# Making the low parts of the weights on GpSimd beside the scans, in a two-layer hybrid encoder

## The chip, the cores and the metric

The kernel runs on one core of a Trainium2 chip. The metric is the device time of one execution in microseconds (us); three runs of the kernel before took 1644.47 to 1645.33 us, with a median of 1645.07 us. Lower is better.

## The reference, cut to what matters

A sequence of 512 positions with 1024 features goes through two layers. Each layer does this:

```
h = rmsnorm(x, norm1_g[i])
u = h @ w_in[i]
q, k, v, z, xbc, dt_raw, sc_b, sc_c, sc_x = split(u)
a_out = attention_mixer(q, k, v, ...)          # 8 heads, dilated windows
s_out = ssd_mixer(z, xbc, dt_raw, ...)         # 16 heads, two directions, chunks of 128
c_out = short_conv_mixer(sc_b, sc_c, sc_x, ...)
x = x + concatenate([a_out, s_out, c_out]) @ w_out[i]
x = x + conv_ffn(rmsnorm(x, norm2_g[i]), ...)  # silu(gate) * val, 2816 wide
```

The SSD mixer ends with a gate and a norm over each of two groups of heads, and the sum of squares of a group is taken over 512 features:

```
y = y.reshape(b, s, SSD_GROUPS, gsz) * silu(z).reshape(b, s, SSD_GROUPS, gsz)
y = y * rsqrt(mean(y * y, axis=-1) + EPS)
```

All of it is float32. The kernel computes the large products in three passes of a faster format: each operand is split into a high part (rounded) and a low part (what the rounding leaves), and high x high, high x low and low x high are summed.

## The kernel before, in words

Weights come in chunks of 128 x 1024 (512 KB), 128 of them a layer and a small one (dt), in one fixed order (CHUNKS): qk, dt, v, xbc, sc, z, o1 (first half of the output projection), o2 (second half), up, dn. Raw chunks W, high parts WHI and low parts WLO have two buffers each, taken in turn. SyncE loads chunk n when the low part of chunk n-2 is made. ScalarE makes the high part of chunk n+2 (L525) when TensorE has used chunk n (`high_after`). Another engine then makes the low part, raw minus high, and counts it in the semaphore w_lo. TensorE waits for w_lo before a chunk's first matmul and then runs 24 matmuls of 512 columns, three for each of 8 blocks (L1168 to L1170).

The 28 chunks sc, z and o1 are the slots 0 to 27 (SLOTS). Beside them the scans of the SSD run, and each engine's program goes through the slots in the same order and places pieces of the scan there by slot number. Each engine is an in-order queue: an instruction that waits holds up all behind it. The pieces that matter here:

- sc slots 0 to 11: three slots make one tile of the short convolution. VectorE adds two taps (L1093, on SBUF alone), multiplies (L1069, L1071), ScalarE makes the product's high part (L710) and GpSimd its low part (L488) in slots 2, 5, 8 and 11.
- Scan groups start in slots 2 and 13. TensorE turns the group's tiles into token order, ScalarE copies them out (L734), GpSimd scales them (`scale_states`, L462, two in each of three slots), TensorE makes states of them (L1318).
- Heads: DMA brings a head's rows, ScalarE makes the decays (`head_exp`, L609, L612), VectorE weighs them (L915) and adds the two directions (L920, on SBUF alone) in slots 4 to 11 and 15 to 22. TensorE uses two heads at a time (`within`, L1330), in slots 6, 8, 10, 12, 17, 19, 21 and 23. After it VectorE combines (`combine`, L924, L931, L932) and GpSimd adds the backward part (`add_backward`, L467).
- z slots 12 to 19: VectorE evacuates z tile i into one of four buffers (L1078); from z4 on it waits until GpSimd's `gate` (L472) of tile i-4 has read that buffer. Gates 0 and 1 stand in slot 16, 2 and 3 in slot 17, 4 to 6 in slots 20 to 22, 7 in slot 24.
- Sums of squares: GpSimd adds four squared tiles to one (`sum_squares`, L450 and L452), for group 0 in slot 24 and for group 1 in slot 27. TensorE sums over the partitions (L1217): for group 0 after slot 25, and for group 1 within the first o2 chunk, between its two halves.

In all other chunks GpSimd makes the low part (L437). In the 28 slots VectorE makes it (L845), at the place of `low_after` in VectorE's slot loop: after the evacuation and the weighing, before `combine` and the taps. In GpSimd's loop over o2 the first low part waits for the last one of VectorE.

Of the kernel before, what the change touches and what calls it, by code (L numbers as in the profile page):

```python
# [8 lines left out]
F32, F32R = mybir.dt.float32, mybir.dt.float32r  # L9
ACT, ALU = mybir.ActivationFunctionType, mybir.AluOpType  # L10
# [56 lines left out]
NCH = len(CHUNKS)  # L67
POS = {c: i for i, c in enumerate(CHUNKS)}
# [76 lines left out]
def build_trunk(nc, a):  # L145
    ctx = ExitStack()
    now = [0]

    def sb(name, shape, dt=F32):
        return ctx.enter_context(nc.sbuf_tensor(f"sb_{name}", shape, dt))  # L150
# [13 lines left out]
    def sem(name, per=0):  # L164
        return Count(ctx.enter_context(nc.semaphore(name)), per, now)
# [6 lines left out]
    W = sb("w_raw", [P, 2, CHUNK])  # L172
    WHI = sb("w_hi", [P, 2, CHUNK], F32R)
    WLO = sb("w_lo", [P, 2, CHUNK], F32R)
# [80 lines left out]
    w_hi, w_lo, w_used = sem("w_hi", NCH), sem("w_lo", NCH), sem("w_used", NCH)  # L255
# [54 lines left out]
    def direction_chunk(j):  # L310
        d, i = j % 2, j // 2
        return d, (i if d == 0 else QT - 1 - i)
# [116 lines left out]
    def _(pool):  # L429
# [9 lines left out]
        def low_after(kind, i):  # L439

            n = now[0] * NCH + POS[kind, i] + 2
            if (kind, i) == ("o2", 0):
                pool.wait_ge(w_lo.handle, n)
            if n < DEPTH * NCH:
                w_low(n)

# [7 lines left out]
        def scale_states(n):  # L454
            grp, j = n // 6, n % 6
            d, c = direction_chunk(j)
            col = column(d, 8 * grp)
            pool.wait_ge(*ws_done.at(1))
            pool.wait_ge(*tok_copied.at(5 * grp + 5))
            if j >= 2:  # L460
                pool.wait_ge(*st_mm.at(n - 1))
            g.tensor_tensor(SQ[:, j % 2, :].rearrange("p (h e) -> p h e", e=64), XT[:, c, :].rearrange("p (h e) -> p h e", e=64),  # L462
                            WS[:, c, col:col + 8].unsqueeze(2).to_broadcast([P, 8, 64]), ALU.mult).then_inc(xs_done.handle, 1)
# [12 lines left out]
        for layer in range(DEPTH):  # L476
            now[0] = layer
            for pos in range(POS["sc", 0]):
                low_after(*CHUNKS[pos])
                if layer == 0 and CHUNKS[pos] == ("qk", 2):  # L480
                    pool.wait_ge(bias_row.handle, 2)
                    g.dma_start(scratch[:, :, :], rm["bias_row"][:, :].unsqueeze(1).to_broadcast([HEADS, COPIES, REL]))\
                        .then_inc(bias_stored.handle, 16)
            for s, (kind, i) in enumerate(SLOTS):
                if kind == "sc" and i % 3 == 2:
                    t = i // 3
                    pool.wait_ge(*sc_hi.at(t + 1))
                    g.tensor_tensor(rm["ml_sc"][:, t, :], SCP[:, :], rm["mh_sc"][:, t, :].bitcast(F32), ALU.subtract)\  # L488
                        .then_inc(sc_lo.handle, 1)
                for grp in range(SSD_GROUPS):  # L490
                    if 0 <= s - GROUP_AT[grp] < 3:
                        for j in range(2):
                            scale_states(6 * grp + 2 * (s - GROUP_AT[grp]) + j)
                if s in PAIR_AT:
                    add_backward(PAIR_AT[s])
                if s in (16, 17):
                    gate(2 * (s - 16))
                    gate(2 * (s - 16) + 1)
                if s in (20, 21, 22):
                    gate(s - 16)  # L500
                if s == 24:
                    gate(7)
                if s in (24, 27):
                    sum_squares((s - 24) // 3)
            for m in range(KT):
                low_after("o2", m)
            for j in range(2 * FF_T):
                low_after("up", j)
                if j % 2 == 1:
                    t = j // 2  # L510
                    pool.wait_ge(*ff_hi.at(t + 1))
                    g.tensor_tensor(FLO[:, t, :], FP[:, :], FHI[:, t, :].bitcast(F32), ALU.subtract).then_inc(ff_lo.handle, 1)  # L512
            for i in range(DOWN_C * KT):
                low_after("dn", i)
# [290 lines left out]
    def _(dve):  # L805
        v = nc.vector
# [30 lines left out]
            v.scalar_tensor_tensor(mixed("l", 8 + t), XC[:, t, :], par(PA_SNG + t), mixed("h", 8 + t).bitcast(F32),  # L837
                                   ALU.mult, ALU.subtract).then_inc(y_lo.handle, 1)

        def low_after(kind, i):  # L840

            n = now[0] * NCH + POS[kind, i] + 2
            dve.wait_ge(w_hi.handle, n + 1)
            dve.wait_ge(w_lo.handle, n)
            v.tensor_tensor(WLO[:, n % 2, :], W[:, n % 2, :], WHI[:, n % 2, :].bitcast(F32), ALU.subtract).then_inc(w_lo.handle, 1)  # L845

        def root_ready(name):
            dve.wait_ge(*root_done.at(NORMS.index(name) + 1))

# [101 lines left out]
        for layer in range(DEPTH):  # L951
# [81 lines left out]
            for s, (kind, i) in enumerate(SLOTS):  # L1033
# [19 lines left out]
                b, n = TILE_BANK[kind, i]  # L1053
# [28 lines left out]
                if s in WEIGH_AT:  # L1082
                    weigh(WEIGH_AT[s])
                    add_directions(WEIGH_AT[s])
                low_after(kind, i)
                if s in PAIR_AT:
                    combine(PAIR_AT[s])
                if kind == "sc" and i % 3 == 1:
# [16 lines left out]
            for m in range(KT):  # L1105
                b1, n1 = TILE_BANK["o1", m]
                dve.wait_ge(*evac[b1].at(n1 + 1))
                for half in range(2):
                    b, n = TILE_BANK["o2", 2 * m + half]
# [18 lines left out]
            for j in range(2 * FF_T):  # L1128
                t, col = j // 2, PA_FF + 4 * j
                b, n = TILE_BANK["up", j]  # L1130
# [14 lines left out]
            for m in range(KT):  # L1145
                b, n = TILE_BANK["down", m]
# [419 lines left out]
```

## Time and profile before

| | |
|---|---|
| median of 3 runs | 1645.07 us |
| profiled execution | 1644.51 us (span 1642.6 us) |
| TensorE matmul busy | 1621.8 us, 99% |
| VectorE busy | 910.4 us, 55% |
| ScalarE busy | 763.3 us, 46% |
| GpSimd busy | 645.7 us, 39% |
| granted TensorE clock | 1.000 |

Busy time over span gives the share of each engine. The slots of the first layer lie between 209 and 409 us of the span, those of the second 812 us later. In that stretch (212 to 412 us) VectorE is busy 138.73 us of 200, ScalarE 125.57 and GpSimd 51.01. In the views below, a row of the timeline has its start, its length, the engine, the line and the operation with its shapes. The bracket at its end is the idle time of the engine before it, and what ended it. The times of consecutive rows of one instruction form (x2) are merged.

### The profile page before, as it was taken

What the parts mean: (1) busy time and instruction counts of PE and PEld (TensorE: products, weight loads), DVE (VectorE), ACT (ScalarE), POOL (GpSimd) and SP (SyncE); (2) the same over time, 40 slices, a digit from 0 to 9 for tenths busy, and PEclk for the clock granted to TensorE, in tenths of its full rate; (3) what the DMA queues carried; (4) which work ended last, traced back from release to release, by engine and by line L of the source; (5) the groups of instructions that cost most, each with busy time, mean ns of one, the idle gap of its engine ahead of it and who ended that gap; (6) DMA issues with size and microseconds to landing.
All of it is one profiled execution on the core that took longest, in us unless ns stands there. A gap on an engine that the chain in (4) does not pass through costs nothing.

```text
span 1642.6 us, 19275 instructions
## 1 busy us (share of the span) xinstructions
PE 1621.8 (99%) x7352; PEld 1266.6 (77%) x7352; DVE 910.4 (55%) x1310; ACT 763.3 (46%) x1204; POOL 645.7 (39%) x323
## 2 busy tenths in 40 slices
PE   7999999999999999999999999999999999999999
PEld 5776778787778888888877776787777788888887
DVE  4578858567754545421227778686678455455000
ACT  5456666575343333332244665765734433333221
POOL 3432221224345555554443322213144555555443
PEclk9999999999999999999999999999999999999999
DMA  5532145352223322323324222454523223322333
GB/s 170 133 105 80 52 115 159 126 159 91 91 90 91 102 91 90 98 87 95 93 90 129 87 74 65 129 155 131 153 83 101 91 90 90 97 96 87 96 93 109
DMA packets 57371, 170.86 MB, mean 104 GB/s; under 512 B 5984, under 2 KB 11872, under 8 KB 57280
## 3 DMA queue, kind: packets, MB, share of 16 engines
q1 hardware_dynamic: 56896, 168.88, 33.4%
q0 software_dynamic: 384, 0.75, 0.4%
q8 instruction: 59, 0.97, 0.3%
q14 instruction: 32, 0.26, 0.0%
HBM read 166.24 MB, written 3.38 MB: 103 GB/s over the span
## 4 chain that ended last, share of the span: by engine, by line
PE 85%; DMA 5%; DVE 3%; issue 3%; POOL 2%; ACT 2%; SPq 1%; DVEq 0%; POOLq 0%; ACTq 0%
PE banks L1168 25%; PE banks L1169 25%; PE banks L1170 25%; DMA sb_w_raw<-w_in 3%; PE banks L1246 2%; PE banks L1255 2%; PE banks L1266 2%; DMA sb_e<-sum_rows 1%; PE banks L1318 1%; PE banks L1226 1%; POOL sb_xc L472 1%; DVE sb_w_lo L845 1%; SPq L337 1%; ACT sb_w_hi L525 0%; DVE sb_sc_acc L1093 0%
## 5 line engine op out<-in xcount | busy, mean ns | idle before, releaser
L437 POOL TENSOR_TENSOR sb_w_lo<-sb_w_raw,sb_w_hi 128x1024 fp32r<-128x1024 f32 x200 | 482.4, 2412 | 629.3 <-ACT sb_w_hi L525 629.3
L525 ACT ACTIVATE sb_w_hi<-sb_w_raw 128x1024 fp32r<-128x1024 f32 x256 | 271.3, 1060 | 739.4 <-PE banks L1170 686.6
L1168 PE MATMUL banks<-sb_h_hi,sb_w_hi 128*128 128x512 f32 x1344 | 550.2, 409 | 12.1 <-POOL sb_w_lo L437 10.7
L1169 PE MATMUL banks<-sb_h_lo,sb_w_hi 128*128 128x512 f32 x1344 | 533.4, 397 | 0.0
L1170 PE MATMUL banks<-sb_h_hi,sb_w_lo 128*128 128x512 f32 x1344 | 533.0, 397 | 0.0
L1168 PEld LDWEIGHTS banks<-sb_h_hi,sb_w_hi 128*128 128x128 f32 x1344 | 253.6, 189 | 92.1 <-issue 29.3
L1169 PEld LDWEIGHTS banks<-sb_h_lo,sb_w_hi 128*128 128x128 f32 x1344 | 253.7, 189 | 64.3 <-issue 6.5
L1170 PEld LDWEIGHTS banks<-sb_h_hi,sb_w_lo 128*128 128x128 f32 x1344 | 253.5, 189 | 61.8
L1133 DVE TENSOR_TENSOR banks<-banks,sb_rstd 128x512 f32<-128x512 f32 x88 | 61.5, 699 | 148.9 <-PE banks L1170 139.7
L1168 PE MATMUL banks<-sb_ff_hi,sb_w_hi 128*128 128x512 f32 x352 | 139.6, 396 | 0.0
L1169 PE MATMUL banks<-sb_ff_lo,sb_w_hi 128*128 128x512 f32 x352 | 139.6, 396 | 0.0
L1170 PE MATMUL banks<-sb_ff_hi,sb_w_lo 128*128 128x512 f32 x352 | 139.5, 396 | 0.0
L1148 DVE TENSOR_TENSOR sb_x_stream<-banks,sb_x_stream 128x512 f32<-128x512 f32 x16 | 11.1, 692 | 201.2 <-PE banks L1170 201.2
L845 DVE TENSOR_TENSOR sb_w_lo<-sb_w_raw,sb_w_hi 128x1024 fp32r<-128x1024 f32 x56 | 72.7, 1298 | 25.5 <-ACT sb_w_hi L525 25.4
L1170 PEld LDWEIGHTS banks<-sb_ff_hi,sb_w_lo 128*128 128x128 f32 x352 | 66.3, 188 | 16.2
L1169 PEld LDWEIGHTS banks<-sb_ff_lo,sb_w_hi 128*128 128x128 f32 x352 | 66.3, 188 | 16.2
L1168 PEld LDWEIGHTS banks<-sb_ff_hi,sb_w_hi 128*128 128x128 f32 x352 | 66.3, 188 | 16.2
L512 POOL TENSOR_TENSOR sb_ff_lo<-sb_ff_prod,sb_ff_hi 128x512 fp32r<-128x512 f32 x44 | 56.9, 1292 | 51.5 <-DVE sb_ff_hi L1144 51.5
L868 DVE SCALAR_TENSOR_TENSOR sb_xc<-banks,sb_params,sb_xc 128x509 f32<-128x509 f32 (+2 forms) x96 | 71.9, 749 | 5.5 <-ACT sb_xc L582 2.6
L467 POOL TENSOR_TENSOR sb_xc<-sb_xc,sb_t_normed 128x384 f32<-128x384 f32 x16 | 18.9, 1183 | 139.0 <-DVE sb_xc L932 139.0
L894 DVE CUSTOM_DVE_ANT_0 sb_scores<-banks,sb_bias_t 128x512 f32<-128x512 f32 x64 | 41.5, 685 | 33.0 <-PE banks L1246 33.0
L1135 DVE SCALAR_TENSOR_TENSOR sb_ff_val<-banks,sb_params,sb_ff_val 128x511 f32<-128x511 f32 x44 | 33.0, 750 | 46.2 <-ACT sb_ff_val L786 46.2
(206 smaller groups left out, 2220.5 us busy)
## 6 DMA issues: line engine op xcount, KB each, us to landing
sb_w_raw<-w_in SPq DMA_DIRECT2D x88, 512.0 KB, 3.7
sb_w_raw<-w_up SPq DMA_DIRECT2D x88, 512.0 KB, 3.6
sb_w_raw<-w_out SPq DMA_DIRECT2D x32, 512.0 KB, 3.6
sb_w_raw<-w_down SPq DMA_DIRECT2D x32, 512.0 KB, 3.5
sb_e<-sum_rows SPq DMA_DIRECT2D x16, 512.0 KB, 6.1
sb_bias_t<-bias_rows SPq DMA_DIRECT2D x16, 448.0 KB, 5.9
sb_exp_cs<-sum_rows SPq DMA_DIRECT2D x32, 192.0 KB
sb_w_raw<-w_down SPq DMA_DIRECT2D x16, 384.0 KB, 3.2
```

The source lines that it names most:

```text
L437: g.tensor_tensor(WLO[:, n % 2, :], W[:, n % 2, :], WHI[:, n % 2, :].bitcast(F32), ALU.subtract).then_inc(w_lo.handle, 1)
L512: g.tensor_tensor(FLO[:, t, :], FP[:, :], FHI[:, t, :].bitcast(F32), ALU.subtract).then_inc(ff_lo.handle, 1)
L525: sc.activation(WHI[:, n % 2, :], W[:, n % 2, :], ACT.Copy).then_inc(w_hi.handle, 1)
L845: v.tensor_tensor(WLO[:, n % 2, :], W[:, n % 2, :], WHI[:, n % 2, :].bitcast(F32), ALU.subtract).then_inc(w_lo.handle, 1)
L868: ins = v.scalar_tensor_tensor(acc[:, lo:hi], src[:, lo + o:hi + o], par(PA_CONV7 + 8 * n + t), acc[:, lo:hi], ALU.mult, ALU.add)
L894: v.tensor_tensor_reduce(S[:, u % 2, :], bank(2 + u % 2), BIAS[:, h % 4, at:at + SEQ], scale=-1.0, scalar=3e38, op0=ALU.add, op1=ALU.min, ...
L1133: v.tensor_tensor(bank(b), bank(b), RSTD, ALU.mult).then_inc(up_scaled.handle, 1)
L1135: step(v.scalar_tensor_tensor(acc[:, 1:SEQ], BANK[:, b, 0:SEQ - 1], par(col), acc[:, 1:SEQ], ALU.mult, ALU.add))
L1168: mm(out, whi, hhi, start=start, stop=False)
L1169: mm(out, whi, hlo, start=False, stop=False)
L1170: return mm(out, wlo, hhi, start=False, stop=stop)
L1246: ins = mm(bank(2 + u % 2), qs[hs, h // 2, P * qt:P * qt + P], ks[hs, h // 2, :], start=n == 0, stop=n == 2)
```

## The change

In the 28 slots GpSimd makes the low parts, with the same subtraction. VectorE's function for it and its call go. In GpSimd's slot loop the call stands after the short convolution's low part (sb_ml_sc) and the state scalings, and ahead of `add_backward`, of the gates and of the sums of squares. The wait of GpSimd for VectorE's last low part goes too, since all low parts are now counted by one engine.

```diff
@@ gpsimd
         def low_after(kind, i):
 
             n = now[0] * NCH + POS[kind, i] + 2
-            if (kind, i) == ("o2", 0):
-                pool.wait_ge(w_lo.handle, n)
             if n < DEPTH * NCH:
                 w_low(n)
@@
                         for j in range(2):
                             scale_states(6 * grp + 2 * (s - GROUP_AT[grp]) + j)
+                low_after(kind, i)
                 if s in PAIR_AT:
                     add_backward(PAIR_AT[s])
@@ vector
-        def low_after(kind, i):
-
-            n = now[0] * NCH + POS[kind, i] + 2
-            dve.wait_ge(w_hi.handle, n + 1)
-            dve.wait_ge(w_lo.handle, n)
-            v.tensor_tensor(WLO[:, n % 2, :], W[:, n % 2, :], WHI[:, n % 2, :].bitcast(F32), ALU.subtract).then_inc(w_lo.handle, 1)
-
@@
                     weigh(WEIGH_AT[s])
                     add_directions(WEIGH_AT[s])
-                low_after(kind, i)
                 if s in PAIR_AT:
                     combine(PAIR_AT[s])
```

Line numbers of the changed kernel are up to two lower on GpSimd (L450 is L448 there) and up to ten lower on VectorE and after it. First the GpSimd queue from slot 0 to slot 5 of the first layer, before (sb_w_lo is a low part of weights, sb_ml_sc the short convolution's low part, sb_squares a scaled state; x18 and x20 begin in the chunks before the slots):

```order
L437 TENSOR_TENSOR sb_w_lo<-sb_w_raw,sb_w_hi 128x1024 x18
L488 TENSOR_TENSOR sb_ml_sc<-sb_sc_prod,sb_mh_sc 128x512
L462 TENSOR_TENSOR sb_squares<-sb_x_tok,sb_state_weights 128x512 x6
L488 TENSOR_TENSOR sb_ml_sc<-sb_sc_prod,sb_mh_sc 128x512
L467 TENSOR_TENSOR sb_xc<-sb_xc,sb_t_normed 128x384
```

And the same place in the changed kernel:

```order
L437 TENSOR_TENSOR sb_w_lo<-sb_w_raw,sb_w_hi 128x1024 x20
L486 TENSOR_TENSOR sb_ml_sc<-sb_sc_prod,sb_mh_sc 128x512
L460 TENSOR_TENSOR sb_squares<-sb_x_tok,sb_state_weights 128x512 x2
L437 TENSOR_TENSOR sb_w_lo<-sb_w_raw,sb_w_hi 128x1024
L460 TENSOR_TENSOR sb_squares<-sb_x_tok,sb_state_weights 128x512 x2
L437 TENSOR_TENSOR sb_w_lo<-sb_w_raw,sb_w_hi 128x1024
L460 TENSOR_TENSOR sb_squares<-sb_x_tok,sb_state_weights 128x512 x2
L437 TENSOR_TENSOR sb_w_lo<-sb_w_raw,sb_w_hi 128x1024
L486 TENSOR_TENSOR sb_ml_sc<-sb_sc_prod,sb_mh_sc 128x512
```

A low part now follows each pair of scaled states, and the one of slot 5 follows the second sb_ml_sc. Next GpSimd's queue from the second group's scaled states to gates 2 and 3, slots 13 to 17, before (sb_xc with sb_z is a gate, sb_xc with sb_t_normed an add_backward, sb_sq_ssd the sums of squares):

```order
L462 TENSOR_TENSOR sb_squares<-sb_x_tok,sb_state_weights 128x512 x6
L472 TENSOR_TENSOR sb_xc<-sb_xc,sb_z 128x512 x2
L467 TENSOR_TENSOR sb_xc<-sb_xc,sb_t_normed 128x384
L472 TENSOR_TENSOR sb_xc<-sb_xc,sb_z 128x512 x2
```

The same place in the changed kernel, from the last two scaled states on (slots 15 to 17):

```order
L460 TENSOR_TENSOR sb_squares<-sb_x_tok,sb_state_weights 128x512 x2
L437 TENSOR_TENSOR sb_w_lo<-sb_w_raw,sb_w_hi 128x1024 x2
L470 TENSOR_TENSOR sb_xc<-sb_xc,sb_z 128x512 x2
L437 TENSOR_TENSOR sb_w_lo<-sb_w_raw,sb_w_hi 128x1024
L465 TENSOR_TENSOR sb_xc<-sb_xc,sb_t_normed 128x384
L470 TENSOR_TENSOR sb_xc<-sb_xc,sb_z 128x512 x2
```

The low parts of slots 15 and 16 stand ahead of gates 0 and 1. Last, slots 24 to 27 on GpSimd, before:

```order
L472 TENSOR_TENSOR sb_xc<-sb_xc,sb_z 128x512
L450 TENSOR_TENSOR sb_sq_ssd<-sb_sq_ssd 128x1024
L452 TENSOR_TENSOR sb_sq_ssd<-sb_sq_ssd 128x512
L450 TENSOR_TENSOR sb_sq_ssd<-sb_sq_ssd 128x1024
L452 TENSOR_TENSOR sb_sq_ssd<-sb_sq_ssd 128x512
```

And in the changed kernel:

```order
L437 TENSOR_TENSOR sb_w_lo<-sb_w_raw,sb_w_hi 128x1024
L470 TENSOR_TENSOR sb_xc<-sb_xc,sb_z 128x512
L448 TENSOR_TENSOR sb_sq_ssd<-sb_sq_ssd 128x1024
L450 TENSOR_TENSOR sb_sq_ssd<-sb_sq_ssd 128x512
L437 TENSOR_TENSOR sb_w_lo<-sb_w_raw,sb_w_hi 128x1024 x3
L448 TENSOR_TENSOR sb_sq_ssd<-sb_sq_ssd 128x1024
L450 TENSOR_TENSOR sb_sq_ssd<-sb_sq_ssd 128x512
```

One low part stands ahead of gate 7 and the first sum of squares, and three (slots 25, 26 and 27) between the two sums.

## Rows read from the trace of the kernel before

**Rows 1.** TensorE's waits over the span: total us, times, longest

```profile
PE banks L1168 <- POOL sb_w_lo L437: 10.7, 2, 10.0
PE banks L1217 <- POOL sb_sq_ssd L452: 2.9, 2, 1.7
PE banks L1330 <- DVE sb_squares L920: 1.3, 2, 0.8
```

**Rows 2.** The page's part 5: the two lines that make low parts

```profile
L437 POOL TENSOR_TENSOR sb_w_lo<-sb_w_raw,sb_w_hi 128x1024 fp32r<-128x1024 f32 x200 | 482.4, 2412 | 629.3 <-ACT sb_w_hi L525 629.3
L845 DVE TENSOR_TENSOR sb_w_lo<-sb_w_raw,sb_w_hi 128x1024 fp32r<-128x1024 f32 x56 | 72.7, 1298 | 25.5 <-ACT sb_w_hi L525 25.4
```

**Rows 3.** Timeline of GpSimd and VectorE, slot 22: start us, us

```profile
378.57 2.98 POOL L472 TENSOR_TENSOR sb_xc<-sb_xc,sb_z 128x512 f32<-128x512 f32 x2
380.35 2.29 DVE L845 TENSOR_TENSOR sb_w_lo<-sb_w_raw,sb_w_hi 128x1024 fp32r<-128x1024 f32 x1
```

**Rows 4.** Timeline of GpSimd, ScalarE and TensorE, end of slot 27

```profile
404.48 2.92 POOL L450 TENSOR_TENSOR sb_sq_ssd<-sb_sq_ssd 128x1024 f32<-128x1024 f32 x1 [8.49 <-ACT sb_sq_ssd L559]
407.47 1.63 POOL L452 TENSOR_TENSOR sb_sq_ssd<-sb_sq_ssd 128x512 f32<-128x512 f32 x1
408.45 1.06 ACT L525 ACTIVATE sb_w_hi<-sb_w_raw 128x1024 fp32r<-128x1024 f32 x1 [4.05 <-PE banks L1170]
411.05 1.02 PE L1217 MATMUL banks<-sb_sq_ssd,sb_constants 128*128 128x512 f32 x2
```

**Rows 5.** Timeline of ScalarE, GpSimd and TensorE, slots 21 to 25

```profile
371.42 1.04 ACT L525 ACTIVATE sb_w_hi<-sb_w_raw 128x1024 fp32r<-128x1024 f32 x1
382.87 0.51 PE L1168 MATMUL banks<-sb_mh_at,sb_w_hi 128*128 128x512 f32 x1
388.79 1.06 ACT L525 ACTIVATE sb_w_hi<-sb_w_raw 128x1024 fp32r<-128x1024 f32 x1 [3.31 <-PE banks L1170]
389.68 1.29 POOL L472 TENSOR_TENSOR sb_xc<-sb_xc,sb_z 128x512 f32<-128x512 f32 x1
396.04 1.13 PE L1217 MATMUL banks<-sb_sq_ssd,sb_constants 128*128 128x512 f32 x2 [1.66 <-POOL sb_sq_ssd L452]
```

**Rows 6.** Timeline of ScalarE, VectorE and TensorE, slots 16 and 17

```profile
333.06 1.06 ACT L525 ACTIVATE sb_w_hi<-sb_w_raw 128x1024 fp32r<-128x1024 f32 x1
334.36 0.68 DVE L1078 TENSOR_TENSOR sb_z<-banks,sb_rstd 128x512 f32<-128x512 f32 x1
336.20 0.69 DVE L920 TENSOR_TENSOR sb_e<-sb_e 128x512 f32<-128x512 f32 x1
338.59 1.06 ACT L525 ACTIVATE sb_w_hi<-sb_w_raw 128x1024 fp32r<-128x1024 f32 x1 [0.94 <-PE banks L1170]
339.82 1.09 PE L1330 MATMUL banks<-sb_e,sb_x_tok 128*64 128x128 f32 x16
```

**Rows 7.** Timeline of ScalarE, VectorE, GpSimd and TensorE, slots 1 to 4

```profile
224.03 1.06 ACT L525 ACTIVATE sb_w_hi<-sb_w_raw 128x1024 fp32r<-128x1024 f32 x1
226.27 1.53 DVE L1093 SCALAR_TENSOR_TENSOR sb_sc_acc<-sb_sc_cx,sb_params,sb_sc_acc 128x511 f32<-128x511 f32 x2
232.51 2.04 POOL L462 TENSOR_TENSOR sb_squares<-sb_x_tok,sb_state_weights 128x512 f32<-128x512 f32 x2 [0.96 <-ACT sb_x_tok L734]
237.19 0.40 PE L1169 MATMUL banks<-sb_h_lo,sb_w_hi 128*128 128x512 f32 x1
```

**Rows 8.** Timeline of ScalarE and TensorE, slots 8 and 10; second layer's landing

```profile
275.33 1.06 ACT L525 ACTIVATE sb_w_hi<-sb_w_raw 128x1024 fp32r<-128x1024 f32 x1 [4.42 <-DMA sb_w_raw<-w_in]
279.20 0.39 PE L1168 MATMUL banks<-sb_h_hi,sb_w_hi 128*128 128x512 f32 x1
1086.78 1.06 ACT L525 ACTIVATE sb_w_hi<-sb_w_raw 128x1024 fp32r<-128x1024 f32 x1 [3.58 <-DMA sb_w_raw<-w_in]
```

**Rows 9.** Timeline of TensorE, tenth and last matmul; last stretch of the windows

```profile
13.90 0.40 PE L1168 MATMUL banks<-sb_h_hi,sb_w_hi 128*128 128x512 f32 x1
1639.04 0.39 PE L1170 MATMUL banks<-sb_ff_hi,sb_w_lo 128*128 128x512 f32 x1
1642.00:1642.60 0.60, 0.00 (x0) 0.00 (x0) 0.00 (x0) 0.00 (x0) 0.00 (x0) 0.50 0.00 0
```

## The prediction

> **What bounds the kernel now.** I read the page first. TensorE is busy 99% of the span, and the chain that ended last is 85% TensorE. So almost nothing can be won, and what counts is how often TensorE would stand still. Its waits come next [rows 1]: beside 10.0 us before the first matmul, they are 2.9 us on GpSimd's sums of squares (L452) and 1.3 us on VectorE's L920, both in the scans. The change acts only in the 28 slots of a layer in which a projection chunk is computed beside the scans (slots 0 to 11 sc, 12 to 19 z, 20 to 27 o1). I therefore walked GpSimd's new queue through these slots, with the durations of the timeline, and asked at each step whether TensorE would be waiting. In the sc and z slots a chunk takes about 5.6 us, and each low part must be there when its chunk begins, one slot and the scan's matmuls later.
>
> **What the change removes, adds and moves.** Of the 256 chunks, 56 low parts leave VectorE (28 a layer, 1.30 us each by the mean) and go to GpSimd, 2.41 us each [rows 2]. That is 36 us a layer off VectorE and 67 us a layer onto GpSimd. Both engines have room for it on average, and by that alone the answer would be "nothing". What decides is that queues run in order, and GpSimd's queue holds instructions that wait. Two things are new. A low part now stands behind the scan's work on GpSimd, or that work stands behind the low part, which waits for its high part (w_hi), which ScalarE makes only when TensorE is done with the slot. The w_lo waits that go were free of charge. The DMAs are unchanged, but SyncE loads chunk n+2 when low part n is done, so that late low parts make late loads.
>
> **GpSimd and VectorE shut each other out.** GpSimd's two gates ran from 378.57 to 381.55, and VectorE's low part, issued at 380.35, took 2.29 us and ended at 382.64, 1.09 us after the gate [rows 3]. So it did its work only after GpSimd's instruction. Operations with a PSUM operand show no such stretch. The Trainium skill says so too and speaks against the change: by its page "SBUF — State Buffer", section "SBUF: two separate sides", a VectorE instruction with two SBUF inputs and a GpSimd instruction that reads SBUF exclude each other for the whole instruction. The trace agrees, with the 1.09 us. Were it a mere sharing, or nothing, term 3 below would be 0.6 us instead of 2.9 and the first part of term 4 near 0, some 7 us less in all. A GpSimd instruction that holds this for 2.4 us is twice as long a lock as the one removed.
>
> **Term 1, sum of squares of group 1: +5.5 us a layer.** Before, L450 started at 404.48 and L452 ended at 409.10, and TensorE took the sum at 411.05 without waiting [rows 4]. Now three low parts stand ahead of it; the last belongs to slot 27, whose high part starts at 408.45 and ends at 409.51 [rows 4]. Low part 2.4 gives 411.98; then 2.92 and 1.63 with 0.1 between: 416.6. TensorE comes at 411.05: 5.5 us of waiting. I see no cover for it; the second half of the output matmuls stands behind this sum in its queue.
>
> **Term 2, sum of squares of group 0: +3.9 us.** In slot 21 the high part ends at 372.46 [rows 5], the low part on GpSimd at 374.9, and VectorE's L920 waits for it. Then the add_backward behind the combination (2.5 us of VectorE, 1.0 of GpSimd), gate 5 (1.3), L920 of the next head (0.6) and the next low part (2.4) end at about 383.9, where the chunk of slot 24 began at 382.87 [rows 5]: 1.0 us. In slot 24 the high part starts at 388.79, 1.0 later now: 389.8; behind it 1.06, low part 2.4, gate 1.29 [rows 5], then 2.92 and 1.63, and gaps of 0.3: 399.4, with one VectorE instruction let in between (0.7) about 400. TensorE took this sum at 396.04 after 1.66 us of waiting [rows 5]. So +3.9 (bounds 3.3 and 4.3).
>
> **Term 3, the gates: +2.9 us.** Slot 16's low part stands ahead of gates 0 and 1. Its high part ends at 334.12 [rows 6], the low part at 336.6, gate 0 at 337.9. VectorE's evacuation of z4 (334.36 before) waits for gate 0, since both use the same buffer: it starts at 338.0, and L920 of head 9 is issued 1.84 us later, as 334.36 and 336.20 show [rows 6]: 339.8. But the next high part ends at 339.64 [rows 6], so that GpSimd's low part starts at 339.7, a tenth ahead, and shuts L920 out until 342.1; it ends at 342.7. TensorE needs it at 339.82 [rows 6]: 2.9. If VectorE comes first, 340.4, and the term is 0.6. I take 2.9, as GpSimd is a hair earlier, and keep 0.6.
>
> **Term 4, the sc slots: +2.4 us in the first layer, about 1.8 in the second.** In slot 1 the high part ends at 225.09, GpSimd holds until 227.5, and VectorE's two taps (226.27 before) start 1.2 late; behind them are the product, ScalarE's high part of it and its token copies, and then the two state scalings on GpSimd, 232.51 to 234.55 before [rows 7], now to 235.7. The low part of slot 2 stands behind these: 238.2. TensorE then passes its second matmul at 238.5, not 237.19 [rows 7]: +1.35. In slot 8 the chunk lands with the high part at 275.33 [rows 8]; this landing is late because DMA queues are full behind row loads that wait for TensorE, so I shift it by 1.7 with slot 4's delay and SyncE's order. Then 1.06 for the high part, 0.6 for ScalarE's product, 1.3 for the sc low part in front, 2.4 and gaps: 282.4. The chunk began at 279.1 (its second matmul of the next triple is 279.20) and would now begin at 280.6 [rows 8]: +1.85. Of these 3.2 us, 0.8 is taken back where TensorE waited for L920 before [rows 1]. In the second layer the landing is 0.8 earlier against the slots (1086.78 less 812.3 is 274.5 [rows 8]), but its tile before began as late, hence about 1.8. Bounds: 0, if the loads hold TensorE up anyway, and 3.3.
>
> **The clock.** TensorE ran its first matmuls from 10.00 and reached the 0.24 us spacing at 13.90 after nine of them [rows 1, 9]. At that spacing nine take 2.1 us, so a cold start costs 1.8. The last matmul starts at 1639.04, and the granted clock is 0.50 (1.2 GHz of 2.4) in the last stretch, from 1642.0 [rows 9]. So idling of under 3 us can take it down. Terms 1 and 2 make gaps of 5.5 and, with the wait that is there, 4 to 5 us. I charge one drop a layer, 1.8; bounds none and two.
>
> **Sum.** A layer: 5.5 + 3.9 + 2.9 = 12.3; two are 24.6; the sc slots 4.2; two drops 3.6: 32.4 us. What VectorE gains (36 us a layer) hides beside TensorE, apart from the 0.8 counted above. The profiled execution took 1644.51 (span 1642.6), 0.6 below the median of the runs, 1645.07: 1644.5 + 32.4 = 1676.9, against the median 1677. As such a walk on paper tends to count waits that overlap, I name 1676.
>
> **Rivals.**
> A: only the end of the scans costs. The races go to VectorE (0.6), the sc slots are bounded by their loads (0), and the clock holds: 2 x (5.5 + 3.3 + 0.6) = 18.8, 1664. For it: the sc low parts had up to 2 us of room; against: the slot 2 chain has no load in it.
> B: the clock falls in both gaps of each layer, and the terms are at their upper bounds: 2 x (5.5 + 4.3 + 2.9 + 3.3 + 3.6) = 39, 1684.
> C, faster: VectorE was what held TensorE (L920 1.3 us, and its low parts), and its relief reaches TensorE because GpSimd's three low parts are finished before their turn. This decides if the sum of squares of group 1 isn't delayed, by less than 1.9 us: then 2 x 1.1 us are won, 1642. Against it stands rows 4: the high part of slot 27 ends after the old sums did.
> D: nothing moves, 1645: late low parts and sums are all absorbed by TensorE's queue. The same row is against it.
>
> **Chances.** My case 0.60, A 0.20, B 0.14, C 0.03, D 0.03. The range 1660 to 1686 takes in A and B and leaves out C, D and a part of the tails. A change of 0.2% (3.3 us) is about what can be told from none: faster 0.02, same 0.03, slower 0.95.
>
> **What would show it.** The wait of L1217 on GpSimd's L450 line: 5.5 us a layer for group 1 and some 5 for group 0, where all was 2.9 in total. The z4 evacuation on VectorE waits for GpSimd's gate, with L920 of 2 to 3 us behind it. GpSimd's low parts number 256 at 2.4 us, VectorE's are none. TensorE waits for w_lo in slots 4 and 10, 1 to 2 us. After the two sums of a layer matmuls spaced 0.43 us tell of the clock. I am wrong if L1217 waits under 2 us in group 1, or if the low parts of slots 25 to 27 end before the sum begins without delaying it.

## The result, and the profile of the changed kernel

The changed kernel takes 1681.68 us (median of 4 runs, 1678.51 to 1682.47), the kernel before 1644.77 us beside it (median of 4 runs, 1643.22 to 1645.33). The ratio is 1.0223, with an interval of [1.0209, 1.0238]: 36.9 us slower. The prediction named 1676 us and the range 1660 to 1686.

The page's head and its part 1 say at once that nothing is short of capacity:

```profile
span 1680.6 us, 19217 instructions
PE 1636.5 (97%) x7352; PEld 1274.7 (76%) x7352; DVE 883.4 (53%) x1254; ACT 763.7 (45%) x1204; POOL 773.4 (46%) x379
L437 POOL TENSOR_TENSOR sb_w_lo<-sb_w_raw,sb_w_hi 128x1024 fp32r<-128x1024 f32 x256 | 621.7, 2429 | 745.5 <-ACT sb_w_hi L524 745.5
```

GpSimd has all 256 low parts at 2.4 us, as expected (the last row, from part 5, answers to [rows 2]; VectorE's row is gone), and it is still idle for more than half of the span. What changed is how often TensorE stands still. Its waits (engine, line, waited for: total us, times, longest) answer to [rows 1]; line numbers of the changed kernel are 9 lower for TensorE and 2 lower for GpSimd behind the removed wait, and up to 8 lower for VectorE (L920 is L912 there, and L837 is L836):

```profile
PE banks L1159 <- POOL sb_w_lo L437: 18.2, 9, 10.7
PE banks L1208 <- POOL sb_sq_ssd L450: 15.6, 4, 4.4
PE banks L1321 <- DVE sb_e L912: 5.6, 2, 2.8
```

Before these were 10.7, 2.9 and 1.3 us. The new 24.5 us are 12.7 at the sums of squares, 4.3 at the last operation of a head, and 7.5 at low parts. A row of the kernel before has nothing left to answer to it, since VectorE makes no low parts now:

```profile
PE banks L1168 <- DVE sb_w_lo L845: 1.5, 2, 1.1
```

These two waits were in slot 23 of each layer (0.37 and 1.10 us). The new waits stand where the timeline of TensorE has them (start, us, and in brackets the wait ahead; the last row is of the second layer):

```profile
239.07 0.50 PE L1159 MATMUL banks<-sb_h_hi,sb_w_hi 128*128 128x512 f32 x1 [0.89 <-POOL sb_w_lo L437]
283.36 0.50 PE L1159 MATMUL banks<-sb_h_hi,sb_w_hi 128*128 128x512 f32 x1 [1.77 <-POOL sb_w_lo L437]
347.54 1.09 PE L1321 MATMUL banks<-sb_e,sb_x_tok 128*64 128x128 f32 x16 [2.78 <-DVE sb_e L912]
...
407.26 2.08 PE L1208 MATMUL banks<-sb_sq_ssd,sb_constants 128*128 128x512 f32 x2 [3.33 <-POOL sb_sq_ssd L450]
428.37 2.08 PE L1208 MATMUL banks<-sb_sq_ssd,sb_constants 128*128 128x512 f32 x2 [4.44 <-POOL sb_sq_ssd L450]
...
1115.18 0.50 PE L1159 MATMUL banks<-sb_h_hi,sb_w_hi 128*128 128x512 f32 x1 [2.20 <-POOL sb_w_lo L437]
```

Waits alone don't make up 38.0 us, the difference of the two spans. The rest is the clock. These are windows right behind five of those waits (last three columns: granted clock, DMA share, GB/s):

```profile
283.60:287.00 3.40, 3.40 (x10) 2.69 (x10) 3.37 (x2) 3.37 (x10) 3.01 (x2) 0.58 0.79 236
348.90:352.40 3.50, 3.50 (x10) 2.71 (x9) 3.33 (x6) 0.00 (x0) 0.00 (x0) 0.51 0.39 117
407.60:411.00 3.40, 3.40 (x8) 1.99 (x8) 2.91 (x2) 1.60 (x3) 2.36 (x1) 0.58 0.04 5
428.80:432.40 3.60, 3.60 (x8) 2.08 (x8) 0.00 (x0) 1.32 (x2) 0.00 (x0) 0.50 0.00 0
1115.40:1118.80 3.40, 3.40 (x16) 2.72 (x16) 3.37 (x2) 3.37 (x10) 3.07 (x2) 1.00 0.78 238
```

PE is busy in all of the window and still does 8 to 10 matmuls where it does 16 at full clock: it ran at 1.2 GHz instead of 2.4. The last window, behind the wait of slot 10 in the second layer, kept the full clock. How many such stretches there are differs between executions of the same kernel: the mean granted clock of the four was 0.991, 0.992, 0.991 and 0.994, and the time followed it. The profiled one is the slowest of the four (1682.47 us).

To see which step costs what, take the same matmul in both traces and subtract the starts. Where this shift grows, time is lost. For each layer, in us, with the start that the matmul had before:

| place | what grows it | layer 1 | layer 2 | both |
|---|---|---|---|---|
| slots 0 to 13 (199.7 to 301) | waits at slots 4 and 10, less the old wait at L920 (0.9 and 0.7) | 1.99 | 2.94 | 4.9 |
| slot 17 (339.82) | VectorE's L912 is late | 2.85 | 2.86 | 5.7 |
| slots 21 to 25 (up to 396.04) | slot 24's start, sum of group 0, less the old wait for VectorE's low part in slot 23 (0.0 and 1.0) | 1.97 | 1.50 | 3.5 |
| slot 27 (411.05) | sum of group 1 | 4.44 | 4.45 | 8.9 |
| behind those gaps | matmuls at 1.2 GHz | 7.84 | 6.12 | 14.0 |

That is 37.0 us. The table's last row is what remains of the shift when the waits are taken off. Another 1.1 us arises in the first 200 us, ahead of anything that the change touches; the kernels of the experiments have 0.1 to 1.0 there, so it is scatter.

### The profile page after: what moved, and what is told of

Its sections match the earlier page's. It is cut to its first block, busy times and chain, and to the rows that moved or that the text cites. A ratio compares the mean times of both kernels' runs of the same rounds, so it can differ in the third digit from the quotient of the medians.

```text
span 1680.6 us, 19217 instructions
## 1 busy us (share of the span) xinstructions
PE 1636.5 (97%) x7352; PEld 1274.7 (76%) x7352; DVE 883.4 (53%) x1254; ACT 763.7 (45%) x1204; POOL 773.4 (46%) x379
## 4 chain that ended last, share of the span: by engine, by line
PE 85%; POOL 4%; DVE 3%; ACT 3%; issue 2%; DMA 2%; SPq 0%; DVEq 0%; POOLq 0%; ACTq 0%
PE banks L1159 25%; PE banks L1160 25%; PE banks L1161 25%; DMA sb_w_raw<-w_in 2%; POOL sb_w_lo L437 2%; PE banks L1237 2%; PE banks L1246 2%; PE banks L1257 2%; PE banks L1217 1%; PE banks L1309 1%; POOL sb_sq_ssd L448 1%; PE banks L1321 1%; POOL sb_squares L460 1%; PE banks L1335 0%; PE banks L1208 0%
## 5 line engine op out<-in xcount | busy, mean ns | idle before, releaser
L437 POOL TENSOR_TENSOR sb_w_lo<-sb_w_raw,sb_w_hi 128x1024 fp32r<-128x1024 f32 x256 | 621.7, 2429 | 745.5 <-ACT sb_w_hi L524 745.5
L819 DVE SCALAR_TENSOR_TENSOR sb_h_lo<-sb_x_stream,sb_params,sb_h_hi 128x512 fp32r<-128x512 f32 x32 | 50.1, 1589 | 16.5 <-ACT sb_h_hi L535 16.5
L1126 DVE SCALAR_TENSOR_TENSOR sb_ff_gate<-banks,sb_params,sb_ff_gate 128x511 f32<-128x511 f32 x44 | 33.0, 750 | 45.8 <-ACT sb_ff_gate L785 45.8
```

What stands on the lines that cost most here:

```text
L437: g.tensor_tensor(WLO[:, n % 2, :], W[:, n % 2, :], WHI[:, n % 2, :].bitcast(F32), ALU.subtract).then_inc(w_lo.handle, 1)
L819: v.scalar_tensor_tensor(HLO[:, k, :], X[:, k, :], par((PA_N1, PA_N2)[norm] + k), HHI[:, k, :].bitcast(F32), ALU.mult, ALU.subtract).then_ ...
L1126: step(v.scalar_tensor_tensor(acc[:, 1:SEQ], BANK[:, b, 0:SEQ - 1], par(col), acc[:, 1:SEQ], ALU.mult, ALU.add))
```

## The experiments

All times are medians; ratios are to the kernel before, run on the same chip. What an experiment gives back is worked out from the ratios, and each carries an interval of about 0.15%, 2.5 us, on either side. Slots and terms are the prediction's.

**Slot 27's low part behind the sum (term 1).**

```
+                if s != 27:
                     low_after(kind, i)
 ...
                     sum_squares((s - 24) // 3)
+                if s == 27:
+                    low_after(kind, i)
```

> The changed kernel, with the low part of slot 27 behind the sum of squares of group 1 on GpSimd instead of ahead of it. My theory (the sum waits for a low part that can't be made before TensorE is done with slot 27): TensorE's wait of 4.4 us at this sum goes in both layers, with the stretch at 1.2 GHz behind it, 8.4 us a layer of shift against the kernel before; the rest stays. Time about 1665 us, ratio to the kernel before 1.012. Rival (GpSimd is simply too full, and work that is put off comes back later): the wait moves to the low part of the second o2 chunk, and the time falls by less than 4 us.

Measured: 1667.38 us, ratio 1.0151 [1.0135, 1.0166]. TensorE's waits on the sums fall to two of 3.3 us: those of group 1 are gone. Against the change's 1.0223 it gives back 0.72%, 11.8 us, where I expected 16.8. The waits went as expected (4.4 us a layer), but in this trace a half-clock stretch stands behind slot 10 in both layers and a double one behind the first layer's sum of group 0, so that only two of nine stretches are saved.

**Only slot 27's low part on GpSimd, all else as before.**

```
+ON_GPSIMD = (27,)
 ...
+            if slot == len(SLOTS) or slot in ON_GPSIMD:
                 pool.wait_ge(w_lo.handle, n)
 ...
+                if s in ON_GPSIMD:
+                    low_after(kind, i)
 ...
```

VectorE's call stays for all other slots. The further experiments that start from an `ON_GPSIMD` line have the same edit around it.

> The kernel before with one low part a layer (slot 27's) on GpSimd, ahead of the sum of squares of group 1. My theory: that one instruction carries term 1: high part ends at 409.5, low part 2.4, sums 2.34 and 1.26: TensorE waits 4.4 us, and 1.7 more in a half-clock stretch behind; 2 x 6.1 = 12.2, 1657 us, ratio 1.0075. Rival 1: the queue of the three low parts of slots 25 to 27 makes the wait, and one alone costs 0 to 2 us a layer: 1645 to 1649. Rival 2: the clock falls only because of other gaps before it in the layer: 1653.5, ratio 1.0055.

Measured: 1658.04 us, ratio 1.0084 [1.0069, 1.0099], 13.8 us. Two of 256 low parts make more than a third of the whole loss. GpSimd's timeline of this kernel shows why:

```profile
409.05 2.37 POOL L438 TENSOR_TENSOR sb_w_lo<-sb_w_raw,sb_w_hi 128x1024 fp32r<-128x1024 f32 x1 [13.66 <-ACT sb_w_hi L529]
411.39 2.34 POOL L452 TENSOR_TENSOR sb_sq_ssd<-sb_sq_ssd 128x1024 f32<-128x1024 f32 x1
413.80 1.26 POOL L454 TENSOR_TENSOR sb_sq_ssd<-sb_sq_ssd 128x512 f32<-128x512 f32 x1
```

The engine has been idle for 13.66 us, the last 5 of them with the sum's inputs ready (before, the sum began at 404.48 [rows 4]), because the low part stands first in the queue and waits for its high part. The wait at the sum is 4.5 us in each layer, as with all three low parts: rival 1 is out. So is rival 2: no wait of over 1.2 us comes ahead of it in the layer, and the granted clock from 416 to 423 is 0.67.

**Slot 16's low part behind the gates (term 3).**

```
+                if s != 16:
                     low_after(kind, i)
 ...
                     gate(2 * (s - 16) + 1)
+                if s == 16:
+                    low_after(kind, i)
```

> The changed kernel, with gates 0 and 1 ahead of the low part of slot 16. My theory (z4's evacuation waits for gate 0, and L912 behind it is then shut out by the low part of slot 17): TensorE's wait of 2.8 us at L1321 in slot 17 goes in both layers, and the half-clock stretch behind it, together some 4.3 us a layer; time about 1673 us, ratio 1.017. Rival (the wait comes from ScalarE's table loads or the heads' DMA): the wait stays at 2 us or more. If the gap was only filled by slack that another wait takes, the time moves by under 3 us.

Measured: 1673.21 us, ratio 1.0185 [1.017, 1.02]: 6.3 us back, where I expected 8.6. No wait at VectorE's L912 (L915 in this kernel) is left among TensorE's waits.

**Slot 17's low part on VectorE; slot 16's still ahead of the gates.** This separates delay from lock.

```
+ON_GPSIMD = [s for s in range(28) if s != 17]
```

> The change in every slot but 17, whose low part stays on VectorE, behind its product of head 9. This tells the exclusion apart from the mere delay by slot 16's low part, which still stands ahead of gates 0 and 1. My theory: the wait of 2.8 us for VectorE's last operation of head 9 is a lock held by GpSimd's low part of slot 17; without that low part the operation runs as soon as its product is there and TensorE waits 0.3 to 0.9 us; the half-clock stretch behind goes too: 1681.7 - 2 x 2.2 - 2.7 = 1674.6, ratio 1.018. Rival: slot 16's low part ahead of the gates is the whole cause; the wait stays 2.5 us or more and the time 1680 to 1682.

Measured: 1675.82 us, ratio 1.0195 [1.0178, 1.0212]: 4.6 us back, where I expected 7.1, and the interval just touches that of the change. What decides is therefore the trace. In the changed kernel, the same three steps on VectorE and GpSimd are:

```profile
343.44 1.21 DVE L907 TENSOR_TENSOR sb_e<-sb_e,banks 128x1024 f32<-128x1024 f32 x1
344.59 2.34 POOL L437 TENSOR_TENSOR sb_w_lo<-sb_w_raw,sb_w_hi 128x1024 fp32r<-128x1024 f32 x1 [0.61 <-ACT sb_w_hi L524]
344.69 2.79 DVE L912 TENSOR_TENSOR sb_e<-sb_e 128x512 f32<-128x512 f32 x1
```

and in this experiment (VectorE's timeline; L919 and L924 are the L907 and L912 above):

```profile
341.46 1.21 DVE L919 TENSOR_TENSOR sb_e<-sb_e,banks 128x1024 f32<-128x1024 f32 x1
342.70 0.69 DVE L924 TENSOR_TENSOR sb_e<-sb_e 128x512 f32<-128x512 f32 x1
```

GpSimd came 0.10 us ahead, and the 0.69 us operation took 2.79: it ran when GpSimd's was over (344.59 + 2.34 = 346.93, plus 0.55). Without that low part beside it, it takes 0.69, and TensorE's wait falls from 2.8 to 0.7 us in both layers. The rival, mere delay, is out: slot 16's low part only moves VectorE's work next to GpSimd's, and the lock makes the wait. The Trainium skill says in its page "SBUF — State Buffer", section "SBUF: two separate sides", that a VectorE instruction with two SBUF inputs and a GpSimd instruction that reads SBUF exclude each other for the whole instruction. The trace agrees, with 2.79 against 0.69.

**Low parts on VectorE in slots 0 to 15 (term 4).**

```
+ON_GPSIMD = range(16, 28)
```

> Low parts on VectorE in slots 0 to 15 as before, on GpSimd in slots 16 to 27 as after the change: term 4 (the sc slots) taken away alone. My theory: the sc slots cost 3.8 us in layer 1 and 3.0 in layer 2 (shift of TensorE's matmuls between slot 0 and slot 16, with the half-clock stretch behind slot 10), all else stays: 1681.7 - 6.8 = 1675 us, ratio 1.018. Rival: the late low parts of the sc slots only use up slack that the loads of the next slots take anyway, or the gates and sums take it back: 1680 to 1682, ratio 1.022.

Measured: 1673.46 us, ratio 1.018 [1.0165, 1.0196]. TensorE's matmuls have no further shift up to slot 11 (0.97 at 203.47 and at 284.82). The loads didn't take the gain back.

**Sum of group 0 first in slot 24 (term 2).**

```
+                if s == 24:
+                    sum_squares(0)
                 low_after(kind, i)
 ...
-                if s in (24, 27):
-                    sum_squares((s - 24) // 3)
+                if s == 27:
+                    sum_squares(1)
```

> The changed kernel with the sum of squares of group 0 first in slot 24 on GpSimd, all else as in the change: term 2 alone. My theory: TensorE's wait of 3.3 us there and the half-clock stretch behind it (0.5 us) go, 3.8 us a layer of which 1.7 and 1.2 were there before the change: 1681.7 - 7.4 = 1674.3, ratio 1.0185. Rival: the low part of slot 24, now 3.6 us later, is late for the next chunk and the wait comes back there as one on w_lo: 1679 to 1682.

Measured: 1671.37 us, ratio 1.0169 [1.0155, 1.0182]: 8.9 us less than the change, 1.5 more than I expected. TensorE waits for the sum of group 0 nowhere, and the low part behind it isn't late. The surplus is within the interval. The clock may have a part in it: I had counted 0.5 us of slow matmuls behind this wait, the changed kernel lost 1.5 us there in the first layer (407.60 to 411.00 above) and 2.8 in the second, and this trace has six slow stretches where that of the change has nine.

**All three: low parts first in the queue, except slot 16's behind the gates and slot 27's behind the sum.**

```
+                if s not in (16, 27):
+                    low_after(kind, i)
                 if kind == "sc" and i % 3 == 2:
 ...
-                low_after(kind, i)
```

> The changed kernel, with the low part ahead of the short convolution's low part and of the state scalings, behind gates 0 and 1 in slot 16, and behind the sum of squares in slot 27; slot 24 as in the changed kernel. My theory: the waits in slots 4, 10, 17 and at the group 1 sum go, in all about 8.4 + 4.4 + 3.5 us a layer of the 18.5; what stays is the group 0 sum, some 2 us a layer more than before. Time about 1649 us, ratio 1.003. Rival (the exclusion of VectorE by twice as long instructions costs everywhere): 1658 us or more, with new waits on VectorE's lines.

Measured: 1658.17 us, ratio 1.0093 [1.0076, 1.011], 9 us more than I expected. TensorE's timeline has the reasons:

```profile
236.05 1.16 PE L1305 MATMUL banks<-sb_bc 128*128 128x128 f32 x8 [1.00 <-ACT sb_x_tok L738]
262.52 1.09 PE L1326 MATMUL banks<-sb_e,sb_x_tok 128*64 128x128 f32 x16 [1.54 <-DVE sb_e L917]
...
401.41 2.08 PE L1213 MATMUL banks<-sb_sq_ssd,sb_constants 128*128 128x512 f32 x2 [3.33 <-POOL sb_sq_ssd L450]
```

The wait at the sum of group 0 (the last row) was expected to stay. The first two rows are new, 2.5 us in each layer, and with the half-clock stretch behind the sum of group 0 they make up most of the 9 us. With the low parts ahead of the scan's work in slots 2 to 5, chunks are in time, but the steps of the scan run beside GpSimd's low parts. Ahead of the first wait the two taps of the short convolution took 2.28 and 2.76 us beside two low parts, instead of 0.75 each. VectorE's timeline ahead of the second wait shows the stretch, L943 twice with L946 between:

```profile
253.77 2.77 DVE L943 TENSOR_TENSOR sb_t_normed<-sb_s_in,sb_decays 128x512 f32<-128x512 f32 x1
256.57 0.69 DVE L946 TENSOR_TENSOR sb_s_in<-banks,sb_t_normed 128x512 f32<-128x512 f32 x1
257.18 0.68 DVE L943 TENSOR_TENSOR sb_t_normed<-sb_s_in,sb_decays 128x512 f32<-128x512 f32 x1
```

L943 reads two operands in SBUF and took 2.77 us beside a low part, 0.68 without; L946, with one in PSUM, kept 0.69. So what came is the rival that I had named, in its time (1658) and in its sign (a new wait at a line of VectorE), though only in the sc slots. Putting the low parts first takes term 4's waits away and puts others of similar length in their place.

**The gap at the sum of group 1 filled, not shortened.** Five dummy matmuls into the sum's bank stand ahead of TensorE's wait; their result is overwritten.

```
-            pe.wait_ge(*y_tree.at(2 * grp + 2))
 ...
+                for k in range(5):
+                    mm(bank(6), con["ones"], BC[:, k % 4, :], start=True, stop=True)
+            pe.wait_ge(*y_tree.at(2 * grp + 2))
```

> The changed kernel, with five further float32 matmuls (into the bank of the sum, which overwrites them) while TensorE waits for the group 1 sum of squares: 0.86 us each, 4.3 us, about as long as the wait. My theory (idle TensorE loses its clock, and the matmuls behind the wait run at 1.2 GHz): the granted clock stays at 1.00 behind the sum, and 1.5 to 2.9 us a layer come back; time about 1677 us, ratio 1.0195. Rival (the clock falls for some other reason, or such matmuls don't hold it): clock and time stay, or the time rises by up to 0.8 us a layer.

Measured: 1677.12 us, ratio 1.0208 [1.0192, 1.0223], with runs from 1673.44 to 1679.97. In TensorE's timeline the dummies take the place of the wait:

```profile
421.47 4.45 PE L1208 MATMUL banks<-sb_bc,sb_constants 128*128 128x512 f32 x10
426.11 1.13 PE L1210 MATMUL banks<-sb_sq_ssd,sb_constants 128*128 128x512 f32 x2 [0.18 <-POOL sb_sq_ssd L450]
```

and the windows behind it and behind the sum of group 0, which was left as it is:

```profile
404.00:407.40 3.40, 2.29 (x4) 1.19 (x5) 3.40 (x2) 0.20 (x1) 3.40 (x2) 0.58 0.00 0
424.60:430.00 5.40, 5.22 (x19) 3.12 (x18) 0.00 (x0) 1.32 (x2) 1.38 (x2) 1.00 0.10 40
```

The sum comes just as late, but TensorE goes on at 2.4 GHz: it is idling, not the late sum, that brings the clock down. The other traces bear this out: a gap of 4.4 or 4.5 us stands at this sum 12 times in them, each time with a half-clock stretch behind it, and neither of the two filled gaps has one. What that is worth in time is not shown. The ratios differ by 0.15%, 2.5 us, where I expected 4.7, and their intervals overlap. The trace is of the fastest of the four runs (1673.44), in which two gaps of the second layer that were not filled (2.78 and 3.43 us) kept the clock too.

**Before, with the sum of group 0 ahead of gate 7.** No low part is moved.

```
-                if s == 24:
-                    gate(7)
                 if s in (24, 27):
                     sum_squares((s - 24) // 3)
+                if s == 24:
+                    gate(7)
```

> The kernel before, with no low part moved; in slot 24 GpSimd makes the sum of squares of group 0 ahead of gate 7 instead of behind it. My theory: this removes most of the wait of 1.66 and 1.2 us at the scan's first sum: 1642, ratio 0.9982. Rival: gate 7 comes 4 to 5 us later and holds ScalarE's high part of tile 7 and all behind it, so the gain is given back: 1644 to 1646, ratio 1.000.

Measured: 1640.51 us (11 runs), ratio 0.9982 [0.9973, 0.9991]. This is faster than both kernels, by 0.18% against the one before. That one had 2.9 us of waiting there [rows 1], which the order of one queue made. TensorE waits nowhere for the late gate.

**The same, with slot 10's low part alone on GpSimd.**

```
+ON_GPSIMD = (10,)
```

> As the kernel with the sum of squares of group 0 ahead of gate 7, and besides the low part of slot 10 alone on GpSimd: there VectorE's low part waits for a late high part and holds the combination and the product of the next head behind it. My theory: TensorE's wait of 0.76 and 0.6 us in slot 12 goes too: 1640.7, ratio 0.9974. Rival: GpSimd's 2.4 us low part makes the load of the chunk two slots on later by 1.2 us and costs as much as it brings: same time as without it, 1642. A second rival: it makes it slower, 1645, as every low part of the sc slots does in the changed kernel.

Measured: 1640.4 us (11 runs), ratio 0.998 [0.9972, 0.9989]: no difference from the last. The waits on L920 in slot 12 (0.38 and 0.35 us in the trace of the last kernel) are gone, and in the first layer TensorE waits for the low part itself instead:

```profile
293.75 0.50 PE L1173 MATMUL banks<-sb_h_hi,sb_w_hi 128*128 128x512 f32 x1 [0.46 <-POOL sb_w_lo L438]
```

The time is that of the first rival. Its mechanism, a later load, isn't seen: the wait is for the longer low part. Nor is it shown that moving this low part took the waits on L920 away. The two kernels above with GpSimd's low parts in slot 27 alone and in slots 16 to 27 leave slot 10's on VectorE and had at most 0.15 us of them, so these waits also go without such a move.

**GpSimd makes the low parts of slots 12 to 27, its queue in a mended order.** The sum of group 0 stands first in slot 24, slot 16's low part behind the gates, slot 27's behind the sum of group 1.

```
+ON_GPSIMD = range(12, 28)
 ...
+                if s == 24:
+                    sum_squares(0)
+                if s in ON_GPSIMD and s not in (16, 27):
+                    low_after(kind, i)
 ...
+                if s == 27:
+                    sum_squares(1)
+                    low_after(kind, i)
```

> Low parts on VectorE in slots 0 to 11, on GpSimd in slots 12 to 27 (16 a layer, where the change has 28), with GpSimd's queue in another order: the sum of group 0 first in slot 24, slot 16's low part behind the gates, slot 27's behind the sum of group 1. My theory: what the change cost was the order of a queue and the lock it holds in the sc slots; here it costs nothing and VectorE's relief brings nothing beyond what the early sum of group 0 brings alone: 1640 to 1642, ratio 0.998. Rival 1: the lock (16 times 2.4 us a layer instead of 1.2) costs here too, as VectorE's operations stretch: 1646 to 1650, ratio 1.003. Rival 2: the relief of VectorE (21 us a layer) brings more once nothing waits: under 1638.5, ratio below 0.997.

Measured: 1643.02 us (11 runs), ratio 0.9995 [0.9986, 1.0004]. TensorE's waits in this kernel (L929 is the L920 of the kernel before):

```profile
PE banks L1178 <- POOL sb_w_lo L438: 12.9, 5, 10.5
PE banks L1340 <- DVE sb_squares L929: 1.8, 2, 1.0
PE banks L1178 <- DVE sb_h_lo L829: 1.3, 2, 0.7
```

In the order of the change the low parts of slots 16 to 27 alone cost 1.8%; in this order those and four more a layer cost nothing against the kernel before, and about 2 us (0.13%, with intervals that overlap) against the one with the early sum of group 0. This is between my theory and rival 1. The sc slots have no such mended order among the kernels tried: the one that put their low parts first cost 0.93%. TensorE waits for no sum and no gate; what is left are two waits of 0.3 to 1.0 us a layer for low parts in the o1 slots, and one at L929. VectorE has 32 low parts fewer, and none of that reaches TensorE: rival 2 is out.

## Why the prediction was right, and where its sizes were off

The mechanism and its places were right: all the terms of the sum are seen in the trace. Terms 1 to 3 were each removed by the one reordering that they called for, term 4 by giving slots 0 to 15 back to VectorE, and the total was 1681.7 against 1676. The sizes were off in both directions.

- **What bounds it.** TensorE, and what counts is its standing still: confirmed. The prediction's list of TensorE's waits left out 1.5 us for VectorE's own low parts (the row of L845 above), and so a thing that the change could give back. By the shifts 0.9 and 0.7 us came back at L920, where 0.8 was counted for the first layer, and 0.0 and 1.0 in slot 23, where nothing was. How much of this is VectorE's relief stays open: at L920 kernels with VectorE's low parts left in place had waits from 0 to 1.0 us, and in slot 23 kernels with GpSimd's had 0.1 to 1.0.
- **Term 1, +5.5 a layer: 4.44 measured.** The sum began when the walk said (low part at 422.29, 1.1 us behind the start of its high part, which was late with all else). But it then took 2.34 + 1.26 us, where I put 2.92 + 1.63 from [rows 4]. The sizing step failed on a thing that the prediction itself explains elsewhere, the lock. VectorE's timeline of the kernel before, beside the sum from 404.48 to 409.10:

```profile
403.92 1.23 DVE L845 TENSOR_TENSOR sb_w_lo<-sb_w_raw,sb_w_hi 128x1024 fp32r<-128x1024 f32 x1 [0.40 <-ACT sb_w_hi L525]
405.06 2.89 DVE L837 SCALAR_TENSOR_TENSOR sb_ml_ssd<-sb_xc,sb_params,sb_mh_ssd 128x512 fp32r<-128x512 f32 x1
```

VectorE's low part held up the first addition until 405.15, and L837 came in ahead of the second. The change takes the low part away, and L837's operation was long done when the late sum began (416.88). GpSimd's timeline of the changed kernel:

```profile
422.29 2.38 POOL L437 TENSOR_TENSOR sb_w_lo<-sb_w_raw,sb_w_hi 128x1024 fp32r<-128x1024 f32 x1 [3.15 <-ACT sb_w_hi L524]
424.63 2.34 POOL L448 TENSOR_TENSOR sb_sq_ssd<-sb_sq_ssd 128x1024 f32<-128x1024 f32 x1
427.05 1.26 POOL L450 TENSOR_TENSOR sb_sq_ssd<-sb_sq_ssd 128x512 f32<-128x512 f32 x1
```

- **Term 2, +3.9 a layer: 1.97 and 1.50.** The same in slot 24: L448 took 2.37 us, not the 2.92 that I assumed, while L450, which VectorE's L836 still ran beside, took 1.59 as before (1.61); the 0.7 us that I added for a VectorE instruction let in did not come on top of that. Slot 24's start was late by 0.36, not 1.0: the steps that the prediction lists from 374.9 add up to 382.7, and with L920's own 0.7 us to 383.4, not to its 383.9. In the second layer slot 23 gained the 1.0 of the wait for VectorE's low part. The waits at the sum are 3.33 us against 1.66 and 1.2 before.
- **Term 3, +2.9: 2.85 and 2.86.** Right to the tenth, including who wins the race for the lock (GpSimd, by 0.10 us). With a margin so small that is luck as well: the other branch was priced at 0.6, and I took this one because GpSimd was a tenth ahead on paper too. The experiment with slot 17 on VectorE gives the other branch, 0.7 where I had written 0.6.
- **Term 4, +2.4 and 1.8: 1.99 and 2.94.** Slot 4 grew by 1.16 and 1.17 (1.35 forecast), slot 10 by 1.77 and 2.20 (1.85). The wait at L920 took 0.9 and 0.7 of it back.
- **The clock, 1.8 a layer: 7.84 and 6.12.** This is the term that was mis-sized most, by 10.4 us in all. I charged one slow stretch a layer. There were five and four in the profiled execution, 1.55 us each on average: behind slot 10 (first layer only), behind slot 17 and behind both sums, one of which in each layer had a double stretch. Both layers lie above the upper bound of two drops, 3.6. All gaps of 2.78 us and more were followed by one in this trace. Rival B (1684) had priced two a layer and all terms at their upper bounds; its clock was nearer, its terms were not.

So the waits were 5.8 us too dear (28.8 forecast, 23.0 measured), the clock 10.4 us too cheap, and 1.1 us is scatter at the start. That the total came within 6 us is partly these two errors cancelling. Rival A's view that the sc slots are bounded by their loads fell with the experiment that put them back on VectorE. Rivals C and D fell with the waits at the sums, 15.6 us in place of 2.9.

The single removals, by the ratios, give back 11.8 (slot 27), 8.9 (slot 24, of which 2.9 were there before), 7.1 (sc slots) and 6.3 us (slot 16): 34 us, or 31 of the 36.9 that the change added. The rest is within what four ratios with intervals of 0.15% each leave open.

## What to carry to other kernels

Before moving work to an engine with idle time, write down what stands behind it in that engine's queue and how late its input is; a low part of 2.4 us with a late input ahead of one short sum cost 6.9 us a layer, and behind the sum the same work left no wait there. When the moved work used to share a lock with its neighbours, their old durations are no longer theirs: ask for each which two-input operations of the other engine will still stand beside it. And charge the clock for every gap of about 3 us and more, not once a layer: here that was more than any single term.

## What the runs showed of the hardware

The lock works for a whole instruction, in both directions, and it changes hands between waiting engines. GpSimd's and VectorE's timelines of the changed kernel in slots 24 and 25:

```profile
403.17 2.37 POOL L448 TENSOR_TENSOR sb_sq_ssd<-sb_sq_ssd 128x1024 f32<-128x1024 f32 x1
405.62 1.59 POOL L450 TENSOR_TENSOR sb_sq_ssd<-sb_sq_ssd 128x512 f32<-128x512 f32 x1
407.17 2.80 POOL L437 TENSOR_TENSOR sb_w_lo<-sb_w_raw,sb_w_hi 128x1024 fp32r<-128x1024 f32 x1
```

```profile
398.95 0.74 DVE L836 SCALAR_TENSOR_TENSOR sb_ml_ssd<-sb_xc,sb_params,sb_mh_ssd 128x512 fp32r<-128x512 f32 x1
...
404.57 5.94 DVE L836 SCALAR_TENSOR_TENSOR sb_ml_ssd<-sb_xc,sb_params,sb_mh_ssd 128x512 fp32r<-128x512 f32 x3
```

VectorE's L836 with two SBUF inputs takes 0.74 us by itself; three of them took 5.94 beside GpSimd's queue. One by one they ended at 406.08, 407.75 and 410.51, each 0.54 or 0.55 us behind the end of a GpSimd instruction (405.54, 407.20, 409.96). GpSimd's L450 and L437, at 1.26 and 2.38 us undisturbed, took 1.59 and 2.80: each let one of VectorE's in ahead of it. VectorE's operations with an operand in PSUM kept their time beside GpSimd: the 32 instructions of L907 (one input in PSUM) took 1.20 to 1.22 us in the changed kernel, the 32 of L912 (both in SBUF) 0.69 to 2.91.

- The length of a gap doesn't settle alone whether TensorE's clock falls. A wait of 1.77 us was followed by matmuls at 1.2 GHz, and one of 2.20 us at the same place of the second layer was not; nor were 1.66 us before the change. Over the traces of all kernels here, 6 of 15 gaps of 1.5 to 2.2 us were followed by such matmuls, and 33 of 36 gaps of 2.78 to 4.51 us. The three that weren't (2.78, 3.33 and 3.43) are in the second layers of the kernel with the filled gap and of the one with slot 17 on VectorE. Which gap is hit stays open.
- Waits that were filled with matmuls nobody needs kept the clock at 2.4 GHz behind them, both of them in the one trace (granted clock 1.00, where it was 0.50).
